# Low weights 128 bytes off from the high ones, activations in two layouts, one meta key tile, scaling on ScalarE

## What is computed

```
s = einsum('bqhd,bkd->bqhk', q_idx, k_idx)
score = einsum('bqhk,bqh->bqk', relu(s), w_idx * idx_scale)
_, sel = top_k(where(visible, score, NEG_INF), k_top)
p = softmax(where(valid, q @ k[sel] * attn_scale, NEG_INF))
out = p @ v[sel]
...
return x + (g_a * y_a + g_b * y_b) @ w_out
```

## Time and profile before

| | us |
|---|---|
| three runs | 1242.18, 1242.20, 1243.21 (median 1242.2) |
| the profiled execution's own time | 1242.63 |
| its span, first to last instruction | 1240.8 |
| TensorE busy, products (8,794) | 1223.4, 99% |
| TensorE busy, weight loads | 1128.8, 91% |
| VectorE, ScalarE, GpSimd busy | 620.0, 717.6, 979.9 |

### The profile page before, as it was taken

How to read it: one execution, slowest core, us unless ns; L and a number is a source line. 1 busy time by engine, 2 the same in 40 slices (tenths; PEclk the granted TensorE clock), 3 DMA queues, 4 the chain that set the end, 5 groups by cost and what they waited for, 6 DMA issues and landing times.

```text
span 1240.8 us, 22233 instructions
## 1 busy us (share of the span) xinstructions
PE 1223.4 (99%) x8794; PEld 1128.8 (91%) x8794; DVE 620.0 (50%) x1461; ACT 717.6 (58%) x1344; POOL 979.9 (79%) x774
## 2 busy tenths in 40 slices
PE   7999999999999999999999999999999999999998
PEld 6999899998889888889999999999999988888886
DVE  5476754456756444412756678742135235444411
ACT  6455646465556666645645677774447437666642
POOL 5666768767568999989789767779889758898895
PEclk9999999999999999999999999999999999999999
DMA  7334435434335555555456555545556425555552
GB/s 255 137 137 142 148 121 186 153 138 168 113 128 199 189 187 187 189 184 187 158 207 214 180 167 181 181 160 187 178 179 224 167 104 183 206 187 186 185 184 106
DMA packets 59911, 213.31 MB, mean 172 GB/s; under 512 B 6656, under 2 KB 6944, under 8 KB 59680
## 3 DMA queue, kind: packets, MB, share of 16 engines
q1 hardware_dynamic: 57456, 207.67, 48.0%
q10 hardware_dynamic: 2352, 4.23, 1.2%
HBM read 210.79 MB, written 1.08 MB: 171 GB/s over the span
## 4 chain that ended last, share of the span: by engine, by line
PE 96%; DVE 2%; ACT 1%; DMA 0%; issue 0%; SPq 0%; DVEq 0%
PE bank L388 19%; PE bank L361 18%; PE bank L362 17%; PE bank L363 17%; PE bank L391 10%; PE bank L1474 2%; PE bank L1473 2%; PE bank L1472 2%; PE bank L905 1%; PE bank L709 1%; PE bank L915 1%; PE bank L1920 1%; PE bank L847 1%; PE bank L2278 1%; PE bank L2280 1%; PE bank L2279 1%
## 5 line engine op out<-in xcount | busy, mean ns | idle before, releaser
L321 POOL TENSOR_TENSOR wlo<-raw,whi 128x512 fp32r<-128x512 f32 x770 | 979.7, 1302 | 248.1 <-ACT whi L313 246.6
L313 ACT ACTIVATE whi<-raw 128x1024 fp32r<-128x1024 f32 x387 | 405.1, 1053 | 54.1 <-DMA raw<-w_dram 29.5
L361 PE MATMUL bank<-xx,whi 128*128 128x256 f32 (+1 forms) x1296 | 377.3, 291 | 8.4 <-DVE xx L454 8.4
L362 PE MATMUL bank<-xx,whi 128*128 128x256 f32 (+1 forms) x1296 | 368.7, 284 | 0.0
L363 PE MATMUL bank<-xx,wlo 128*128 128x256 f32 (+1 forms) x1296 | 367.7, 284 | 0.0
L361 PEld LDWEIGHTS bank<-xx,whi 128*128 128x128 f32 x1296 | 246.1, 190 | 15.1 <-issue 11.0
L362 PEld LDWEIGHTS bank<-xx,whi 128*128 128x128 f32 x1296 | 245.6, 189 | 1.5 <-issue 1.0
L363 PEld LDWEIGHTS bank<-xx,wlo 128*128 128x128 f32 x1296 | 245.1, 189 | 0.0
L388 PE MATMUL bank<-xx,whi 128*128 128x512 f32 x704 | 177.2, 393 | 0.0
L388 PEld LDWEIGHTS bank<-xx,whi 128*128 128x128 f32 x704 | 126.5, 189 | 22.6
L361 PE MATMUL bank<-yy,whi 128*128 128x256 f32 (+1 forms) x502 | 145.0, 289 | 0.0
(11 more groups left out here) (292 smaller groups left out, 1520.6 us busy)
## 6 DMA issues: line engine op xcount, KB each, us to landing
raw<-w_dram SPq DMA_DIRECT2D x387, 512.0 KB, 3.3
ar<-sums_dram ACTq DMA_DIRECT2D x16, 256.0 KB, 3.9
ar<-mem_dram SPq DMA_DIRECT2D x1, 1024.0 KB, 6.3
out_dram<-ar SPq DMA_DIRECT2D x4, 256.0 KB, 2.2
cst<-con_dram SPq DMA_DIRECT2D x1, 721.0 KB, 9.1
h<-x_dram SPq DMA_DIRECT2D x2, 272.0 KB, 4.6
h<-x_dram SPq DMA_DIRECT2D x1, 544.0 KB, 5.9
ar<-fin_dram SPq DMA_DIRECT2D x1, 512.0 KB, 4.3
```

The lines of the kernel that those rows point to most:

```text
L313: e.activation(whi[:, i % NSPL, :], raw[:, i % NRAW, :], ACT.Copy).then_inc(*whi_done.done(i))
L321: return e.tensor_tensor(wlo[:, q, c0:c1], raw[:, i % NRAW, c0:c1], whi[:, q, c0:c1].bitcast(F), ALU.subtract)
L361: e.matmul(o, wh, both[:, 0, :], start=(i == 0), stop=False)
L362: e.matmul(o, wh, both[:, 1, :], start=False, stop=False)
```

## The change

1. `wlo` gets 64 floats more and its slots begin 32 floats (128 bytes) in. As 64 floats are 256 bytes, what is allocated after it keeps its remainder.
2. The low copy in `yy` is 6176 floats on, in mx and x 2336 and in n1 2208 (128 bytes more than a multiple of 256), in n0 2192 (64 bytes more). f2 takes f1's 288 and 2304. Hidden chunks of the FFN stand even ones first, odd ones 12 x 256 + 32 floats on; the heads' outputs of the cross-attention stand 288 apart. The last FFN and the memory's norm keep a view `ys` with 6144.
3. The meta keys of a head are no longer a tile. Their probabilities for all eight heads are gathered into one tile `LM` (128 queries by 8 x 16), transposed once, and multiplied with `VZ`, which holds the meta values of each head in its own 64 columns and zeros elsewhere. `VZ` is made once a layer by a product and a VectorE multiplication. `PT` holds a pair of heads and has one buffer instead of two.
4. The multiplication with the reciprocal goes from VectorE to ScalarE, two instructions a head.

```diff
-YCOLS = 24 * 256
-XCOLS = 5376
+YCOLS = 24 * 256 + 32
+XCOLS = 4672
...
+    raw, whi, wlo = tens["raw"], tens["whi"], tens["wlo"][:, 32:32 + NSPL * SLOT].rearrange("p (a b) -> p a b", a=NSPL)
+    yy, ys = (tens["yy"][:, 0:2 * n].rearrange("p (a x) -> p a x", a=2) for n in (YCOLS, YCOLS - 32))
...
-        "n0": Norm("n0", "ng0", rows[0], cols3[0], 0, h, xx, T),
-        "n1": Norm("n1", "ng1", rows[1], cols3[1], 0, h, xx, T),
+        "n0": Norm("n0", "ng0", rows[0], cols3[0], 0, h, *stepped(T, 8 * T + 16)),
+        "n1": Norm("n1", "ng1", rows[1], cols3[1], 0, h, *stepped(T, 8 * T + 32)),
...
-        "mx": Norm("mx", "mxn", rows[1], cols3[1], Z, h, *stepped(288, 2368), Z),
-        "x": Norm("x", "xn", rows[0], cols3[0], Z, h, *stepped(320, 2592), Z),
-        "f2": Norm("f2", "f2n", rows[1], cols3[1], Z, h, *stepped(320, 2688), Z),
+        "mx": Norm("mx", "mxn", rows[1], cols3[1], Z, h, *stepped(288, 2336), Z),
+        "x": Norm("x", "xn", rows[0], cols3[0], Z, h, *stepped(288, 2336), Z),
+        "f2": Norm("f2", "f2n", rows[1], cols3[1], Z, h, *stepped(288, 2304), Z),
...
-            return c0, nk, [(2, 0, 16), (0, 16, 128)] + ([(1, 144, 128)] if t else [])
+            return c0, nk, [16, 144][0:t + 1]
...
+                for i in range(nn):
+                    for q in range(2):
+                        m = e.matmul(ob[64 * q:64 * q + 64, 128 * j:128 * j + 128], K.V[:, i, 0:64], pt[:, nn * q + i, :],
+                                     start=(i == 0 and j == 0), stop=False, skip_group_check=True)
...
+            if s == 7:
+                e.wait_ge(*v_step.of("vz", l))
+                e.wait_ge(*s_out.of("pm", l, t))
+                for j in range(4):
+                    m = e.matmul(ob[:, 128 * j:128 * j + 128], K.VZ[:, 128 * j:128 * j + 128], K.PM, start=False, stop=True,
+                                 skip_group_check=True)
...
+            for hh in (2 * s - 4, 2 * s - 3) if 2 <= s < 6 else ():
+                x, r = K.L[:, hh, META:nk], K.rs[:, hh:hh + 1]
+                e.wait_ge(*v_step.of("rs", l, t, s - 2))
+                e.activation(x, x, ACT.Copy, scale=r).then_inc(*s_step.done("p", l, t, hh))
+                if t:
+                    e.wait_ge(*piece.of("pm", l, 0))
+                e.activation(K.LM[:, META * hh:META * hh + META], K.L[:, hh, 0:META], ACT.Copy, scale=r).then_inc(
+                    *s_step.done("lm", l, t, hh))
...
-                e.wait_ge(*v_step.of("rs", l, t, s - 2))
-                for hh in (2 * s - 4, 2 * s - 3):
-                    x = K.L[:, hh, 0:nk]
-                    e.tensor_scalar(x, x, K.rs[:, hh:hh + 1], None, ALU.mult).then_inc(*v_step.done("p", l, t, hh))
...
-        return yy[:, :, i * S:(i + 1) * S]
+        at = i // 2 * S + i % 2 * (12 * S + 32)
+        return yy[:, :, at:at + S]
...
+            self.y = y_both if nxt else lambda j: ys[:, :, j * S:(j + 1) * S]
...
-            "wlo": sb("wlo", [128, NSPL, SLOT], R), "h": sb("h", [128, 8, T]),
-            "xx": sb("xx", [128, XCOLS], R), "yy": sb("yy", [128, 2, YCOLS], R),
+            "wlo": sb("wlo", [128, 64 + NSPL * SLOT], R), "h": sb("h", [128, 8, T]),
+            "xx": sb("xx", [128, XCOLS], R), "yy": sb("yy", [128, 2 * YCOLS], R),
```

More of the change, by code:

```diff
@@ L35 @@
 C_EPS64 = 1708
-NCONST = 1710
+C_REP, C_HM = 1710, 1838
+NCONST = 1846
 PARAMS = {}
@@ L87, in constants @@
     c[:, C_EPS64] = 64 * EPS
+    c[p % 16, C_REP + p] = 1.0
+    c[p, C_HM + p // 16] = 1.0
     c[:, C_EPS] = EPS
@@ L770, in values_tensor @@
         yield
+        o = side_.take(e, "vz", l)
+        side_.give(("vz", l), (v_step, ("vz", l)))
+        e.wait_ge(*s_out.of("vm", l))
+        e.matmul(o[:, 0:64], cst[0:META, C_REP:C_REP + 128], K.V[0:META, 2, 0:64], start=True, stop=True).then_inc(
+            *piece.done("vz", l))
+        yield
     def values_vector(e, K):
@@ L893, in attend_tensor @@
         l = K.l
-        c0, nk, kcs = K.keys(t)
-        nn = len(kcs)
+        c0, nk, firsts = K.keys(t)
+        nn = len(firsts)
         for s in range(8):
@@ L899, in attend_tensor @@
             if s >= 4:
-                pair = (2 * s - 8, 2 * s - 7)
-                e.wait_ge(*s_out.of("pt", l, t, pair[1]))
-                for i, (vi, _, kn) in enumerate(kcs):
-                    for hh in pair:
-                        half = 64 * (hh % 2)
-                        m = e.matmul(ob[half:half + 64, 128 * (hh // 2):128 * (hh // 2) + 128], K.V[0:kn, vi, 0:64],
-                                     K.PT.at(l, t, hh)[0:kn, i, :], start=(i == 0), stop=(i == nn - 1),
-                                     skip_group_check=True)
-                        if i == nn - 1:
-                            m.then_inc(*piece.done("av", l, t, hh))
@@ L910, in attend_tensor @@
-            for hh in (range(2 * s - 6, 2 * s - 4) if 3 <= s < 7 else ()):
-                o = side_.take(e, "pT", l, t, hh)
-                side_.give(("pT", l, t, hh), (s_out, ("pt", l, t, hh)))
-                e.wait_ge(*v_step.of("p", l, t, hh))
-                for i, (_, k0, kn) in enumerate(kcs):
-                    m = e.transpose(o[0:kn, 128 * i:128 * i + 128], K.L[:, hh, k0:k0 + kn], ident)
-                m.then_inc(*piece.done("pT", l, t, hh))
+                j = s - 4
+                e.wait_ge(*s_out.of("pt", l, t, j))
@@ new lines, in attend_tensor @@
+            if 3 <= s < 7:
+                j = s - 3
+                o = side_.take(e, "pT", l, t, j)
+                side_.give(("pT", l, t, j), (s_out, ("pt", l, t, j)))
+                for q in range(2):
+                    e.wait_ge(*s_step.of("p", l, t, 2 * j + q))
+                    for i, k0 in enumerate(firsts):
+                        at = 128 * (nn * q + i)
+                        m = e.transpose(o[:, at:at + 128], K.L[:, 2 * j + q, k0:k0 + 128], ident)
+                m.then_inc(*piece.done("pT", l, t, j))
@@ L917, in attend_tensor @@
+            if s == 6:
+                o = side_.take(e, "pm", l, t)
+                side_.give(("pm", l, t), (s_out, ("pm", l, t)))
+                e.wait_ge(*s_step.of("lm", l, t, 7))
+                e.transpose(o[:, 0:128], K.LM, ident).then_inc(*piece.done("pm", l, t))
             for hh in (2 * s, 2 * s + 1) if s < 4 else ():
@@ L950, in attend_vector @@
         l = K.l
-        c0, nk, kcs = K.keys(t)
+        c0, nk, _ = K.keys(t)
         bs = K.scr[t][:, 0:nk]
@@ L1469, in last_tile @@
     def last_tile(e, K, q, t, o, j, wh, wl, ends, both):
-        yhj, ylj = (y[:, S * j + 128 * t:S * j + 128 * t + 128] for y in (yh, yl))
+        yhj, ylj = (K.y(j)[:, i, 128 * t:128 * t + 128] for i in range(2))
         e.wait_ge(*v_low.of("hid", K.key, j))
@@ L1548, in ffn_tensor @@
             return
-        src = [(y_both(j), ("hid", K.key, j)) for j in range(22)]
+        src = [(K.y(j), ("hid", K.key, j)) for j in range(22)]
         norm_begin(e, K.nxt)
@@ L2248, in build @@
     NQ = norms["x"]
-    NM = Norm("mem", "mn", rows[1][:, 0:S], cols3[1], 0, mem_sb, yy[:, :, 0:8 * S], S)
+    NM = Norm("mem", "mn", rows[1][:, 0:S], cols3[1], 0, mem_sb, ys[:, :, 0:8 * S], S)
     MEM_AT = {4: (0, 1), 5: (2, 3), 6: (4, 5), 7: (6, 7)}
@@ L2394, in cross_tensor @@
             tick(side)
-        srco = [(y_both(8 + j), ("xo", j // 2)) for j in range(8)]
+        srco = [(yy[:, :, 8 * S + 288 * j:8 * S + 288 * j + S], ("xo", j // 2)) for j in range(8)]
         norm_begin(e, norms["f2"])
```

71 lines of the change are left out of this document (44 added, 27 removed).

## The result

The changed kernel takes 1234.53 us (median of 4 runs, 1234.41 to 1234.63) against 1242.29 before (4 runs, 1242.18 to 1243.21): a ratio of 0.9935, 95% interval 0.9919 to 0.9950, 7.8 us less. The profiled execution took 1234.55 us, span 1232.5. The forecast was 1233.8 us, with a range of 1217 to 1240.5.

A forecast was written before the change was run, and what follows sets the result against it. TensorE's own sequence, busy 99% of the span, was taken as the bound. Attention -3.8, scaling -1.6 and addresses -3.4 summed to -8.8 us, taking 1242.6 to 1233.8 us, range 1217 to 1240.5.

The forecast's parts named there:

- Part 1: Attention on TensorE: without the separate meta-key tile, fewer transposes and cheaper weighted sums, -3.8 us.
- 28 fewer at 0.11 us, -3.1: Attention transposes on TensorE: 80 become 48 plus 4 of the meta probabilities, -3.1 us.
- Part 2: Scaling moved to ScalarE: wait near 307 us shrinks, -0.9 us; half the clock loss goes, -0.7; together -1.6 us.
- The wait at 342.5: TensorE's wait of 0.58 us at 342.54 us for scaled probabilities: nothing won.
- ScalarE at nothing: ScalarE's extra 7.5 us per layer in the attention, costed at nothing, covered by slack and weights split ahead.
- rival 2: ScalarE becomes late in the second query tile; waits and clock losses make the kernel slower, 1248.1 us; chance 0.1.
- Part 3: Addresses of low weights and activations: narrow products start closer together, -3.4 us.
- The term of -0.7 us for constant phases: 450 narrow products on yy with constant phase now alternate, going from 119.9 to about 118.4 ns: -0.7 us.
- The term of -2.7: Some 5,000 other narrow products on xx and yy gain 0.55 ns each as high and low alternate: -2.7 us.
- wide 0: Wide stretches of both feed-forwards: shifted low weights and the second one's new layout change nothing, 0.
- Rival 1: Addresses give much: 2.2 to 6.5 ns on 5,000 narrow products, total 1205 to 1226 us; chance 0.2.
- Rival 3: Addresses give nothing or take a little, narrow stretches keeping their pace: 1237.2 to 1240.7 us; chance 0.25.

The follow-up runs named there:

- scaling alone: Kernel before with the multiplication by the reciprocal moved to ScalarE, one instruction a head, meta keys still a tile: 1239.42 us, ratio 0.9977.
- addresses alone: Kernel before with all address edits (xx, yy and the low weights) and the old attention: 1240.02 us, ratio 0.9985.
- the last kernel: Changed kernel with only the 32 scalings of 16 columns (meta copies) put back on VectorE: 1236.37 us, ratio 0.9952.
- offset alone: Kernel before with nothing but the low weights' buffer begun 128 bytes later: 1243.65 us, ratio 1.0012.
- tile alone: Kernel before with the meta keys' separate tile removed as in the change, scaling left on VectorE, old addresses: 1244.79 us, ratio 1.0021.

## Why the prediction was right, and where not

The total was right within 0.7 us, made of steps that were off in both directions.

**Part 1, -3.8 us: mis-sized.** Counts were as forecast: 52 transposes, 128 passes of sums. With scaling already on ScalarE the tile is worth 1239.42 - 1237.34 = 2.1 us (2.6 by the spans). The term that failed is "28 fewer at 0.11 us, -3.1": added up from start to start, the transposes went from 8.92 us (scaling alone) to 6.77 in the change, 2.15 us; those left over are 0.14 us apart and no longer 0.11. They come in smaller groups, each with a wait of its own, which may be why; no run tells. The sums saved more than the 0.7 us forecast, 13.49 to 12.30 us, what makes `VZ` included. 0.4 us went in the mixer, as said under the table. And the step had no condition: with scaling on VectorE the tile costs 2.6 us.

**Part 2, -1.6 us: mis-sized, 3.15 measured.** The wait near 307 us went from 1.43 to 0.6 with the move alone, as computed, and to 0.3 in the change. What the prediction did not see is why the multiplications took so long: they waited out GpSimd's subtractions, as shown above. The wait at 342.5 was to stay and fell to 0.3, then 0.2. The larger part is the clock: I took half of its 1.5 us, and the whole went from the trace (layer 1's first tile 50.28 to 47.95, of which 0.8 is the wait); the second tile gave 0.7. That event is not bound to the wait, though: the kernel with the addresses alone waited 1.4 us there too, at clock 1.00 behind it.

**ScalarE at nothing: right but for 0.2 us of waits**, and rival 2 had the right place. Its chance of 0.1 was low for a margin of about a twentieth.

**Part 3, -3.4 us: near in size (2.55 alone, 2.8 on top of the attention), but not for the reasons given.** The term of -0.7 us for constant phases was a little too small: those products fell by 2.2 ns (120.0 to 117.8), not 1.5. The term of -2.7 was argued from high and low weights alternating. The narrow products do gain by it, 2.3 us, but the offset that makes them alternate takes as much elsewhere, where the sum had nothing, and gives nothing in total. What stays in the total are the activations' layouts. The reading of the earlier trace rows was also coarser than it looked. The mean distances of all the mixer's products before, by place in the pattern of six, are 116 and 117 ns at two places and 119 to 120 at the other four, not 113 at one and 119.5 at five. In the change they are 117 at three places and 118 to 119 at three:

```profile
691.08 0.28 PE L366 MATMUL bank<-xx,whi 128*128 128x256 f32 x1
691.20 0.28 PE L367 MATMUL bank<-xx,whi 128*128 128x256 f32 x1
691.32 0.28 PE L368 MATMUL bank<-xx,wlo 128*128 128x256 f32 x1
691.43 0.28 PE L366 MATMUL bank<-xx,whi 128*128 128x256 f32 x1
...
691.79 0.28 PE L366 MATMUL bank<-xx,whi 128*128 128x256 f32 x1
```

Six products in 0.71 us, 118.3 each. Two costs had been left out or set at nothing: "wide 0" (ffn 1 up +0.28, within its own scatter, ffn 2 up -0.29 us), and the last projection, not costed, +0.56. The three parts were off by +1.7, -1.5 and +0.7 us or so, and that the sum came within 0.7 us of the measured time is in part luck.

**Rivals.** Rival 1 fell: no stretch came under 117 ns. Rival 3 fell as a whole, since the addresses gave 2.55 to 2.8 us. It holds for the offset. By the Trainium skill ("SBUF — State Buffer", section "Who interferes with whom") TensorE's two read ports are independent and it never waits on anyone. That is a rule on engines in each other's way and says nothing of addresses; that placing buffers alters nothing was the prediction's reading of it. That reading does not hold: the last projection takes 59.6, 60.2 to 60.8 or 61.1 us for the same products by where the operands lie.

## What to carry to other kernels

Price a move of work between engines together with the edit beside it: here the tile cost 2.6 us with scaling on VectorE and gave 2.1 with it on ScalarE, and only a kernel for each corner shows that. A tiny instruction on VectorE is not always a short one: before adding 32 multiplications, look what GpSimd does at the time, since here they took 0.22 us beside an idle GpSimd and up to 1.28 in the tile's kernel beside a busy one. Where products are bound by their own pace, lay out streamed and stationary operands by stage and compare stage by stage, because the same 128 bytes gave 0.4 us in one and took 0.6 in another. And compare the granted clock of the two traces first: one fall is some 1.5 us here, more than several of the edits.

## What was not expected of the hardware

- The pace of an unchanged product depends on where its operands lie: in the last projection 226 to 227 ns with all addresses equal modulo 256 bytes and 232 with streamed and stationary ones 128 apart; but narrow products 120.0 with all equal and 117.8 in the change. Equal is best for the one and worst for the other. Why is not settled, and in the mixer and in ffn 1 there is a second influence, of like size, with no address changed.
- A VectorE multiplication of 16 columns took 483 ns on average in one kernel and 735 in another, up to 1.35 us, and 297 on ScalarE. It takes 0.22 us alone, and one that begins while GpSimd subtracts lasts until GpSimd is done.
- A wait of 1.4 to 1.5 us was followed by some 4 us at a granted clock of 0.57 in two traces, before and the last kernel, and by 1.00 in three others with the same wait (addresses alone, offset alone, tile alone, which has 0.60 behind a later wait of 2.07 us and 1.00 behind one of 1.85). A wait of 0.6 to 0.7 us at 17 us was followed by a fall in all four traces that have it, one of 0.6 us at 72 us in none of the fourteen. What decides is open.
